# Exponentials placed ahead of the last queries, two subtractions moved to GpSimd, and expert numbers found by exclusive or and minimum

## The reference

```python
s = einsum('thpc,hpnc->thpn', (x @ wq).reshape(T, 8, 2, 128), subkeys)
s1, i1 = top_k(s[:, :, 0], 16)
s2, i2 = top_k(s[:, :, 1], 16)
cand = (s1[..., :, None] + s2[..., None, :]).reshape(T, 8, 256)
sc, ci = top_k(cand, 16)
expert = i1[ci // 16] * 128 + i2[ci % 16]
gate = softmax(sc)
hpre = einsum('tkd,td->tk', u_tab[expert], x)
y = einsum('tk,tkd->td', gate * gelu(hpre), v_tab[expert])
```

## Time and profile before

| | |
|---|---|
| median of the timed runs | 2156.04 us (2153.06 to 2158.79, n = 3) |
| profiled execution, its own time | 2147.0 us |
| span of the profiled execution | 2145.2 us |
| busy: PE, DVE, POOL, ACT | 1622.2, 1335.1, 1022.3, 398.1 us |
| moved by DMA | 718.93 MB, mean 335 GB/s |
| first gather of u rows | 490.0 us after the start of the span |

### The profile page before, as it was taken

One profiled execution on the slowest core, in us unless ns is written; L12 is line 12 of the kernel. 1 busy time (PEld: TensorE's weight loads), 2 busy tenths in 40 slices (PEclk: granted clock), 3 DMA queues, 4 the chain that ended last, 5 costly groups with the idle time before them and its releaser, 6 DMA issues. The chain is left out here.

```text
span 2145.2 us, 32147 instructions
## 1 busy us (share of the span) xinstructions
PE 1622.2 (76%) x12789; PEld 967.1 (45%) x12789; DVE 1335.1 (62%) x2994; ACT 398.1 (19%) x754; POOL 1022.3 (48%) x1093
## 2 busy tenths in 40 slices
PE   7998979899978795597887656988886656655564
PEld 7887866765655561165665302565552001100000
DVE  4286178785545458774545778655457865776745
ACT  1321332242222011122401201232012001000000
POOL 0000020004745455665545566655455777777774
PEclk9997999998989896598999756999887555555555
DMA  9214285657999999999999999999999999999996
GB/s 255 79 49 135 82 225 177 223 192 259 384 374 399 399 401 411 376 374 373 399 399 400 415 401 376 385 367 398 399 400 406 388 402 407 407 406 403 403 407 270
DMA packets 271256, 718.93 MB, mean 335 GB/s; under 512 B 29219, under 2 KB 77822, under 8 KB 270074
## 3 DMA queue, kind: packets, MB, share of 16 engines
q0 software_dynamic: 151904, 554.59, 66.7%
q1 hardware_dynamic: 116552, 161.44, 21.9%
q10 hardware_dynamic: 2650, 0.85, 0.2%
HBM read 695.58 MB, written 21.30 MB: 334 GB/s over the span
## 5 line engine op out<-in xcount | busy, mean ns | idle before, releaser
L2540 DVE CUSTOM_DVE_ANT_0 arena<-arena,ps 128x1024 f32<-128x1024 f32 x520 | 634.5, 1220 | 505.6 <-PE ps L2593 312.6
L2434 POOL DMA_INDIRECT arena<-peer_u_dram,arena x520 | 503.3, 968 | 480.5 <-DVE arena L2540 394.6
L2483 POOL DMA_INDIRECT arena<-peer_v_dram,arena x520 | 490.1, 942 | 163.8 <-issue 153.0
L2593 PE MATMUL ps<-arena 48*128 48x512 bf16 x1040 | 262.2, 498 | 321.5 <-DVE arena L2540 317.9
L1323 PE MATMUL ps<-arena 128*128 128x128 f32 (+1 forms) x3072 | 418.1, 292 | 91.3 <-DMA arena<-w_in_dram 35.9
L1323 PEld LDWEIGHTS ps<-arena 128*128 128x128 f32 x3072 | 382.8, 201 | 182.5 <-issue 121.0
L2608 PE MATMUL ps<-arena 128*32 128x512 f32 x2080 | 394.0, 841 | 23.1 <-DMA arena<-peer_v_dram,arena 22.8
L2593 PEld LDWEIGHTS ps<-arena 48*128 48x128 bf16 x1040 | 53.4, 97 | 633.2 <-DVE arena L2540 563.3
L2574 ACT ACTIVATE arena<-arena 128x4 f32<-128x4 f32 x130 | 26.8, 206 | 901.9 <-DVE arena L2540 901.5
L387 PE MATMUL ps<-arena 128*128 128x260 f32 (+1 forms) x704 | 131.3, 349 | 3.9 <-ACT arena L465 3.9
L387 PEld LDWEIGHTS ps<-arena 128*128 128x128 f32 x704 | 116.2, 193 | 17.9 <-ACT arena L465 4.0
(11 more groups left out here) (368 smaller groups left out, 1795.9 us busy)
## 6 DMA issues: line engine op xcount, KB each, us to landing
arena<-w_in_dram SPq DMA_DIRECT2D x40, 1024.0 KB, 13.0
arena<-peer_wq_dram SPq DMA_DIRECT2D x32, 1024.0 KB, 15.2
arena<-w_out_dram SPq DMA_DIRECT2D x16, 1024.0 KB, 16.3
arena<-w_in_dram SPq DMA_DIRECT2D x30, 512.0 KB, 4.1
arena<-peer_u_dram,arena POOLq DMA_INDIRECT x520
arena<-peer_v_dram,arena POOLq DMA_INDIRECT x520
arena<-w_branch_a_dram SPq DMA_DIRECT2D x8, 1024.0 KB, 15.8
arena<-w_branch_b_dram SPq DMA_DIRECT2D x8, 1024.0 KB, 16.4
```

The costliest lines, as they stand in the source:

```text
L2434: pool.indirect_dma_start(m["arena"][:, at:at + D], None, m["a"]["peer_u"][0], offsets(m, k)).then_inc(m["sem"](f"e_u{k % RU // UB}"), 16)
L2483: pool.indirect_dma_start(e["V"][j % RV], None, a["peer_v"][0], offsets(m, j)).then_inc(v_in[j % RV // BATCH], 16)
L2540: dve.tensor_tensor_reduce(u, u, ps[:, 0:2, :], 1.0, 0.0, ALU.mult, ALU.add, e["hp"][:, c:c + 1]).then_inc(sem("e_h"), 1)
L2593: mm = pe.matmul(ps[:, h, :], e["pick"][r, i:i + 1].to_broadcast([3 * GROUP, P]), e["xp"][r, g % 2, :], start=True, stop=True)
```

## The change

Four things are edited. The first exponentials of tile 0 are placed at a planned time ahead of the copies of the last query columns. The 16 tap copies of v are planned 2 units later. The two subtractions of tile 0 that form the bf16 parts go from DVE to POOL, with a semaphore of their own (first_left); DVE only raises the count that later tiles use. And stage 7 for all tiles works with integers: `keyed` holds the key number with its slot number times 256 in the bits above (`tags`), `pos` holds the wanted slot times 256, their exclusive or has nothing in the upper bits only where the slots agree, so the minimum over 16 is the key number.

```diff
+        if q and n == 0:
+            act.wait_ge(m["sem"]("first_left"), q)
+        elif q:
             wait("left", q)
...
         yield front_at(n, f"left{q}") if n else begins(0) + LEFT_AT[q]
+        if n == 0:
+            dve.sem_inc(F_["left"], 1)
+            continue
...
-        yield at + CHOOSE_PACE[count] * (32 * half + 27) + 0.2
+        yield slab_at(0, 23) + 0.3 if (count, half) == (0, 0) else at + CHOOSE_PACE[count] * (32 * half + 27) + 0.2
...
         if part == 3:
-            link(dve.tensor_copy(topf, topi))
+            if half == 0:
+                link(dve.tensor_scalar(tags, const(m, "iota16"), float(2 * NK), None, ALU.mult))
+            link(dve.tensor_tensor(keyed, topi, tags.unsqueeze(1).to_broadcast([P, 2 * CH, TK]), ALU.bitwise_or))
...
-            st.did(dve.tensor_scalar(pos[:, 0], place, 4, None, ALU.logical_shift_right))
-            st.did(dve.tensor_scalar(pos[:, 1], place, 15, None, ALU.bitwise_and))
+            st.did(dve.tensor_scalar(pos[:, 0], place, 4, 3840, ALU.logical_shift_left, ALU.bitwise_and))
+            st.did(dve.tensor_scalar(pos[:, 1], place, 8, 3840, ALU.logical_shift_left, ALU.bitwise_and))
             settled()
-            link(dve.tensor_copy(posf, pos))
...
-            link(dve.tensor_tensor(one, posf[:, q].unsqueeze(3).to_broadcast(full), iota, ALU.is_equal))
-            link(dve.tensor_tensor(one, one, keys[:, :, q].unsqueeze(2).to_broadcast(full), ALU.mult))
+            link(dve.tensor_tensor(one, pos[:, q].unsqueeze(3).to_broadcast(full), keys[:, :, q].unsqueeze(2).to_broadcast(full), ALU.bitwise_xor))
         else:
-            link(dve.tensor_reduce(pair_ids[:, q], one, AXX, ALU.add))
+            link(dve.tensor_reduce(pair_ids[:, q], one, AXX, ALU.min))
...
     pool.wait_ge(sem("b_unit"), 2)
     spill("gq", lb["conv"]["q"], 1)
+    d = front(m, 0)
+    for q in range(2):
+        m["fs"].wait(pool, 0, "part", q + 1)
+        if q:
+            pool.wait_ge(sem("first_left"), 1)
+        pool.tensor_tensor(d["left"], d["left"] if q else d["x1row"], d["parts"][:, q], ALU.subtract).then_inc(sem("first_left"), 1)
     pool.wait_ge(sem("b_out"), taken(late_number("c", 3)))
     spill("gv", lb["conv"]["v"], 2)
...
-    yield late_at("v", 0) - 0.5
+    yield late_at("v", 0) + 1.5
```

More of the change, by code:

```diff
@@ L155 @@
 PAIRS = WIDE * TK + (TK - WIDE) * NARROW
-CHOOSE = (("top", [P, 2 * CH, TK], F32), ("topi", [P, 2 * CH, TK], U32), ("topf", [P, 2 * CH, TK], F32), ("cand", [P, CH, PAIRS], F32),
-          ("one", [P, CH, TK, TK], F32), ("best", [P, CH, TK], F32), ("besti", [P, CH, TK], U32), ("pos", [P, 2, CH, TK], U32),
-          ("where", [P, CH, TK], U32), ("skip", [P, CH, TK], F32), ("posf", [P, 2, CH, TK], F32), ("pair_ids", [P, 2, CH, TK], F32), ("ex", [P, CH, TK], F32), ("exsum", [P, CH], F32),
+CHOOSE = (("top", [P, 2 * CH, TK], F32), ("topi", [P, 2 * CH, TK], U32), ("keyed", [P, 2 * CH, TK], U32), ("cand", [P, CH, PAIRS], F32),
+          ("one", [P, CH, TK, TK], U32), ("best", [P, CH, TK], F32), ("besti", [P, CH, TK], U32), ("pos", [P, 2, CH, TK], U32),
+          ("where", [P, CH, TK], U32), ("skip", [P, CH, TK], F32), ("tags", [P, TK], U32), ("room", [P, 7, TK], F32), ("pair_ids", [P, 2, CH, TK], F32), ("ex", [P, CH, TK], F32), ("exsum", [P, CH], F32),
           ("ids", [P, PH, TK], F32), ("gates", [P, PH, TK], F32))
@@ L1464, in front_act @@
             act.wait_ge(m["sem"]("b_unit"), 2)
-        if q:
+        if q and n == 0:
+            act.wait_ge(m["sem"]("first_left"), q)
+        elif q:
             wait("left", q)
@@ L1601, in choose @@
     sem = m["sem"]
-    (top, topi, topf, cand, one, best, besti, pos, place, skip, posf, pair_ids, ex, exsum, ids, gates) = (d["choose"][k] for k in (
-        "top", "topi", "topf", "cand", "one", "best", "besti", "pos", "where", "skip", "posf", "pair_ids", "ex", "exsum", "ids", "gates"))
+    (top, topi, keyed, cand, one, best, besti, pos, place, skip, tags, pair_ids, ex, exsum, ids, gates) = (d["choose"][k] for k in (
+        "top", "topi", "keyed", "cand", "one", "best", "besti", "pos", "where", "skip", "tags", "pair_ids", "ex", "exsum", "ids", "gates"))
     work = d["scores"][:, 8 * half:8 * half + 8]
     full = [P, CH, TK, TK]
-    iota = const(m, "iota16").unsqueeze(1).unsqueeze(1).to_broadcast(full)
-    keys = topf.rearrange("p (h q) k -> p h q k", q=2)
+    keys = keyed.rearrange("p (h q) k -> p h q k", q=2)
     pair = (2 * part, 2 * part + 1)
@@ L2212, in running_buffers @@
     f = dict(choose={name: take(shape, dt) for name, shape, dt in CHOOSE}, scores=take([P, HP, NK]))
-    m["e"]["junk"] = f["choose"]["one"].rearrange("p h i j -> p (h i j)")
+    m["e"]["junk"] = f["choose"]["one"].rearrange("p h i j -> p (h i j)").bitcast(F32)
     m["e"]["y"] = flat(f["scores"])[:, 0:D]
```

## The result

The changed kernel takes 2143.32 us (median of 11 runs, 2130.52 to 2150.30) where the kernel before takes 2153.51 us (11 runs beside them, 2139.95 to 2162.88). The ratio is 0.994, with a 95% interval of 0.9916 to 0.9965: faster by 0.6%. My 2150.0 against 2156.04 was a gain of 0.28%, so the direction was right and the size too small.

The account below looks back on a forecast made before the run. The prediction took DMA transfers as the bound from 490 us, and TensorE's order as setting the first gather. 1.45 us (start) + 4.6 (dips) = 6.0 off 2147.0, scaled to timed runs: 2150.0 us, range 2143 to 2157.5.

Parts of the forecast that it names:

- The bound and the two questions: Transfers limit from 490 us; what releases the first gather, and where do saturated transfers fall below their rate?.
- The start: Ahead of the first gather, TensorE's wait on ACT's copy of v vanishes, moving that gather 1.45 us earlier.
- The load of code: GpSimd's code load ahead of its first subtraction: hidden in 26 us of idle time, 0 taken, range 0 to 10.
- DVE's 12.9 us in tile 0: DVE gains 12.9 us in tile 0, choice ready near 474.5, but TensorE's order keeps this from moving the first gather.
- The exclusive or: In each half of a choice, integer passes at float rate save DVE 2.7 us; DVE busy falls to about 1306.
- The dips: Three transfer-rate dips behind choices in the expert stage lose 6.4 us; 5.8 recoverable at most, four fifths taken, 4.6.
- my third window: The third rate dip in the expert stage, 1668 to 1680 us, said to lose 2.2 us.
- The sum: Whole kernel: 1.45 + 4.6 = 6.0 us off, giving 2150.0 us, 0.28% less.
- A: Rival: only the start moves, transfers from 490 us on are a block; 1.45 us, 2154.6; chance 0.18.
- B: Rival: the front gives nothing, code load paid in the first subtraction; only dips gain, 2151.4; chance 0.12.
- C: Rival: start, all dips and the gathers' issue gain, 1.45 + 5.8 + 2 = 9.3 us, 2146.7; chance 0.13.
- D: Rival: slower, through a long GpSimd code load before the first subtraction, up to 12 us, 2168; chance 0.09.

Follow-up runs that it names:

- e2: Kernel before with only the exclusive or, tags and minimum of stage 7, start as before: ratio 0.9973, median 2148.56 us.
- e4: Changed kernel with the two-input exclusive or pass written twice, restoring the old choice length: ratio 0.9998 to before, median 2151.69 us.
- e6: Changed kernel with the one-input minimum pass written twice, restoring the old choice length: ratio 0.9977 to before, median 2148.32 us.
- e13: Changed kernel with the layer norm's square root behind ScalarE's copy and three norm parts four tokens later: ratio 0.9917 to before, median 2136.29 us.
- e12: Kernel before with the layer norm's square root behind ScalarE's copy and three norm parts four tokens later: ratio 0.9937, median 2144.41 us.
- e9: Changed kernel with TensorE's transposes of a choice four tokens later: ratio 0.9941 to before, median 2139.82 us.
- e1: Kernel before with only the tile 0 moves (exponentials early, taps later, subtractions on GpSimd), stage 7 untouched: ratio 0.9979, median 2145.87 us.
- e7: Changed kernel with the exclusive or pass written four times, lengthening each choice: ratio 1.012 to before, median 2175.06 us.

## Why the prediction was right in kind and too small

**The bound and the two questions** held. TensorE's order sets the first gather, and the rate behind choices falls when DVE is late.

**The start** was 1.72 us for 1.45. The rest is the restart of the stream of matmuls: 10.49 and 10.59 us in two pieces, 20.81 in one. The subtraction took 1.99 us (I took 2.4 out of 1.2 to 4.8). The load of code cost nothing that shows: the first subtraction took no longer than the second, and 28.33 us of idle time stood ahead of it. The Trainium skill (GPSIMD Engine Reference, section 2.1, Instruction dispatch) has some 6 us for a first call; no row here shows it, since those 28 us would cover it.

**DVE's 12.9 us in tile 0** moved nothing, as said, and e2 and e4 show it. But "it has its choice ready near 474.5" was wrong, since it came at 480.20. I moved DVE's rows without asking where ACT's second exponentials stand. The answer was behind the tails, and 3.0 us of slack were left, where my 474.5 against 488.59 - 1.45 had 12.6.

**The exclusive or** was priced rightly, with passes of 1.23 and 1.22 us and DVE at 1306.8.

**The dips** are the step that failed in size: "I take four fifths of 5.8, 4.6". Timed at equal clock, the exclusive or is worth 6.4 us (changed against e4 and e6, error 1.0) to 7.7 (before against e2, error 1.3). The traces show two things that the 5.8 left out. Around the three choices the second table has, in the mean over the five kernels with long choices against the six with short ones and unchanged turns, 105.2 against 102.2, 67.9 against 66.2, and 85.8 against 84.5: 3.0 + 1.7 + 1.3 = 6.0 us. And gathers 344 to 352 add 24.2 - 22.5 = 1.7: tile 3's choice delays them ahead of 1668 us, where my third window began. Together that is 7.7 us. At the first choice more than the 2.7 of one half was to be had, since both halves lie beside gathers. The discount for "the turn and the next tile's matmuls" had no row behind it.

"So lost issue time is not won back later" was wrong in part. Between gathers 384 and 440 the kernels with short choices take 148.5 us in the mean, those with long ones 146.0: some 2.5 of the 7.7 us go back, which leaves 5.2. I had called 2.48 us for issuing a pair "hardly quicker" than 2.59 for moving it. But behind tile 3's choice the kernel before issues a u gather every 2.48 us, never held up by more than 0.31 us, while in e13, which had lost less, every second one waits 0.44 to 0.67 us for DVE, and DVE for rows to land:

```profile
1768.72 1.22 DVE L2550 CUSTOM_DVE_ANT_0 arena<-arena,ps 128x1024 f32<-128x1024 f32 x1 [1.95 <-DMA arena<-peer_u_dram,arena]
1770.22 0.94 POOL L2444 DMA_INDIRECT arena<-peer_u_dram,arena  x1 [0.45 <-DVE arena L2550]
1775.34 0.94 POOL L2444 DMA_INDIRECT arena<-peer_u_dram,arena  x1 [0.44 <-DVE arena L2550]
```

The transfers run at 405 GB/s in before and 404 in e13 (1755 to 1792 us), so they limit both. So a kernel that was held up catches up. This is read from the traces, not tried.

**The sum.** 1.72 plus 6.4 to 7.7 is 8.1 to 9.4 us, against 6.0 forecast and 9.3 measured at equal clock, 10 to 12 in the medians of the three series. What the traces place, 1.72 + 5.2, is 6.9, and the rest of the stage is noisy: from gather 0 to 519, without the episode at 270 to 280, the short choices are only 2.8 us ahead in the mean, with an error of 2.6, and at gathers 80 to 96 they are 1.0 us behind (56.1 against 55.1), for a reason not found. Why the timed runs show more is open. One candidate was not tested: the low clock behind gather 270. With the hole in front of it gone, the change is worth 2.2 us at equal clock, 5.2 in the means and 8.1 in the medians (e12 against e13), around the 6.0 forecast. So either the term of the dips was too small, or part of the gain comes through that episode, or both. The 3 us between 6.0 and 9.3 moved the likeliest case over the line of 0.3%, where I had called "no change" the likelier.

**The rivals.** A and B are out, as the dips and the start both gave something. C, at 9.3 us, had the right size by luck: its dips of 5.8 were too small as well, and its 2 us from two-input passes are not there (e6). D did not come.

**What is open.** The low clock behind gather 270 lasted longer (40.5 us for the ten gathers) in six profiles and shorter (30.8 to 32.1) in four. All four profiles of the changed kernel and of the exclusive or alone were among the six, together with those of e4 and e9; before, e1, e6 and e7 were the four. e4 and e6 differ by one pass's kind only and fell on different sides, so neither the choice's length nor the front decides it. What does was not found. In all ten the hole of 3.6 us stood ahead of L892, and in the four profiles without the hole the clock was 1.00 throughout 1380 to 1400 us.

## What to carry to other kernels

In a stage bound by transfers, VectorE's time counts where its work stands between the last product of one token and the release of the next gather; price it from the gathers' own spacing over the whole of each choice, with the number of such places, without a discount that no row supports, and ask how much the gathers catch up behind it: here 2.5 of 7.7 us. Before two profiles are subtracted, lay an untouched instruction of both upon each other, at several places: here 3.65 us of a 5.37 us lead were there ahead of the change, and 8.4 us of a 9.37 us lead were lost in an episode of low clock. The idle hole of TensorE of 3.6 us and what followed cost 5 to 15 us of ten gathers in single profiles, and 12 us (before) or 4 us (changed) of the mean timed run, so a short ACT copy that TensorE waits for belongs ahead of a long one that nobody waits for.

## What the runs showed of the hardware

TensorE's clock can stay at 0.50 while the engine is busy all the time: 20.00 of 20 us at 1380 to 1400 in the changed kernel, in 64x64 matmuls, behind 3.64 us of idle time. Mean clock and time go together over all runs, 16 us for 0.01; which drives the other is not shown.

A VectorE instruction can be held up by a GpSimd one. In e1 the first subtraction on GpSimd ran from 443.02 to 445.01, and a DVE instruction with two inputs of 64 elements, 0.23 us elsewhere, took 1.59:

```profile
443.02 1.99 POOL L1828 TENSOR_TENSOR arena<-arena 128x1024 f32<-128x1024 f32 x1 [26.71 <-ACT arena L1471]
```

```profile
442.25 1.22 DVE L1671 TENSOR_REDUCE arena<-arena 128x64 f32<-128x1024 f32 x1
443.50 1.59 DVE L1673 SCALAR_TENSOR_TENSOR arena<-arena 128x64 f32<-128x64 f32 x1
445.02 0.21 DVE L1676 TENSOR_REDUCE arena<-arena 128x4 f32<-128x64 f32 x1
```

The instruction ended at 445.09, 0.08 us behind the subtraction. By the Trainium skill (SBUF — State Buffer, SBUF: two separate sides) a GpSimd instruction and a DVE instruction with two SBUF inputs exclude each other for the whole of one of them, and this trace agrees, with 1.36 us. For the time of this kernel no effect of the rule could be measured: e4 and e6, which differ by two-input passes, lie 0.7 us apart at equal clock, with an error of 1.6.
